# The first norm of a two-layer backbone kernel: its sums in one round, eight modulation steps ahead of the spread, the third product tile joined to the first two, the power tables moved behind

## What is computed

```python
silu_c, silu_cc = jax.nn.silu(c), jax.nn.silu(c_ctx)
ada_lat = silu_c @ ada_w[l] + ada_b[l]            # shift, scale, gate: 6 x 1024 columns
ada_ctx = silu_cc @ ada_w[l] + ada_b[l]
h = rms_norm(x, lp["ln1"]) * (1.0 + sc1) + sh1    # hc alike, for the context tokens
z = h @ w_in                                      # split into attention, Fourier and S5 parts
...
a_bar = jnp.exp(dt * a)                           # S5: discretised states, 24 groups x 64
b_bar = ((a_bar - 1.0) / a)[..., None] * b
s = associative_scan(a_bar, b_bar u)              # the kernel scans chunks of 8 tokens
```

## Time and profile before

| | before |
|---|---|
| median of 3 runs | 2169.61 us (2168.25 to 2172.53) |
| profiled execution, its own time | 2170.0 us |
| its span | 2168.1 us |
| PE busy | 2125.3 us, 98% of the span |
| DVE busy | 1228.1 us, 57% |
| POOL busy | 903.7 us, 42% |
| ACT busy | 505.2 us, 23% |

### The profile page before, as it was taken

How to read it: one execution, slowest core, us unless ns; L and a number is a source line. 1 busy time by engine, 2 the same in 40 slices (tenths; PEclk the granted TensorE clock), 3 DMA queues, 4 the chain that set the end, 5 groups by cost and what they waited for, 6 DMA issues and landing times.

```text
span 2168.1 us, 30631 instructions
## 1 busy us (share of the span) xinstructions
PE 2125.3 (98%) x12532; PEld 1897.7 (88%) x12532; DVE 1228.1 (57%) x1859; ACT 505.2 (23%) x814; POOL 903.7 (42%) x492
## 2 busy tenths in 40 slices
PE   6999999999999999999999999999999999999998
PEld 4999999877799899999999999888777787888886
DVE  7998981455663546454565424594266757263353
ACT  3115121454300220110201111322265212010010
POOL 2441443200243354444444443455411456766662
PEclk9999999999999999999999999999999999999999
DMA  7363354233553332122233254545310552322331
GB/s 282 100 141 101 116 191 145 88 120 120 199 192 138 133 122 88 59 78 88 78 88 103 92 204 187 120 153 195 127 39 23 197 182 88 107 97 97 97 97 68
DMA packets 105390, 267.80 MB, mean 124 GB/s; under 512 B 22650, under 2 KB 42490, under 8 KB 103470
## 3 DMA queue, kind: packets, MB, share of 16 engines
q1 hardware_dynamic: 68928, 190.87, 25.9%
q10 hardware_dynamic: 36334, 75.07, 10.5%
HBM read 227.56 MB, written 37.88 MB: 122 GB/s over the span
## 4 chain that ended last, share of the span: by engine, by line
PE 89%; DVE 8%; DMA 1%; ACT 1%; issue 1%; SPq 0%; POOL 0%; DVEq 0%; POOLq 0%; ACTq 0%
PE ps L482 67%; PE ps L1062 3%; PE ps L936 2%; PE ps L1076 2%; PE ps L1112 2%; PE ps L600 2%; PE ps L491 2%; DVE t_out L2233 2%; DVE t_in L2233 1%; PE ps L795 1%; PE ps L962 1%; PE ps L974 1%; PE ps L497 1%; PE ps L1009 1%; PE ps L925 1%; DMA ada_first<-in_ada_w 1%
## 5 line engine op out<-in xcount | busy, mean ns | idle before, releaser
L1304 POOL TENSOR_SCALAR whi<-raw 128x1024 fp32r<-128x1024 f32 x244 | 273.5, 1121 | 1212.1 <-PE ps L482 665.3
L1307 POOL TENSOR_TENSOR wlo<-raw,whi 128x1024 fp32r<-128x1024 f32 x244 | 630.7, 2585 | 20.3
L482 PE MATMUL ps<-hh,whi 128*128 128x384 f32 (+1 forms) x1560 | 462.8, 353 | 0.3 <-DVE ada L626 0.3
L482 PE MATMUL ps<-hl,whi 128*128 128x384 f32 (+1 forms) x1560 | 460.0, 351 | 0.0
L482 PE MATMUL ps<-hh,wlo 128*128 128x384 f32 (+1 forms) x1560 | 459.8, 351 | 0.0
L482 PEld LDWEIGHTS ps<-hh,whi 128*128 128x128 f32 x1560 | 283.6, 188 | 21.1 <-ACT mr L1737 1.0
L482 PEld LDWEIGHTS ps<-hl,whi 128*128 128x128 f32 x1560 | 285.3, 188 | 18.6 <-issue 0.2
L482 PEld LDWEIGHTS ps<-hh,wlo 128*128 128x128 f32 x1560 | 285.0, 188 | 18.4
L2166 DVE SCALAR_TENSOR_TENSOR x<-ps,ada,x 128x384 f32<-128x384 f32 (+1 forms) x160 | 80.5, 546 | 335.1 <-PE ps L482 335.0
L482 PE MATMUL ps<-midh,whi 128*128 128x384 f32 (+1 forms) x768 | 231.3, 355 | 1.8 <-DVE midl L2196 1.8
L482 PE MATMUL ps<-midl,whi 128*128 128x384 f32 (+1 forms) x768 | 229.7, 353 | 0.0
(11 more groups left out here) (259 smaller groups left out, 2954.9 us busy)
## 6 DMA issues: line engine op xcount, KB each, us to landing
raw<-in_w_main SPq DMA_DIRECT2D x244, 512.0 KB, 3.3
ada_gap<-in_ada_w SPq DMA_DIRECT2D x40, 512.0 KB, 10.1
ada_mixer<-in_ada_w SPq DMA_DIRECT2D x32, 512.0 KB, 4.0
g_d<-gt ACTq DMA_DIRECT2D x24, 384.0 KB, 2.4
gl<-g_d ACTq DMA_DIRECT2D x8, 1152.0 KB, 6.2
ada_first<-in_ada_w SPq DMA_DIRECT2D x16, 512.0 KB, 15.4
cout_d<-cz SPq DMA_DIRECT2D x12, 512.0 KB, 5.0
cout<-cout_d ACTq DMA_DIRECT2D x6, 1024.0 KB, 9.3
```

The source lines that it names most:

```text
L482: ins = pe.matmul(bank(p, h, a, b), ww[:, w % W_SLOTS, kw * P:(kw + 1) * P], xx[:, kx, a:b], start=(first and i == 0 and j == 0), stop=(la ...
L1304: pool.tensor_scalar(whi[:, u, :], raw[:, u % 2, :], 1.0, 0.0, ALU.mult, ALU.add).then_inc(w_split.sem, 1)
L1307: pool.tensor_tensor(wlo[:, u, :], raw[:, u % 2, :], whi[:, u, :].bitcast(F32), ALU.subtract).then_inc(w_split.sem, 1)
```

## The change

1. `pe_first_sums` takes the place of `pe_sums` for the first norm. DVE adds slice 7 into `sqa` too, so six two-column matmuls are left of twelve.
2. Steps 4 to 7 of the modulation all stand between the sums and the spread (before, two stood ahead of the spread and two behind it). `pe_turn` of block 0 stands between the two matmuls of the spread (`pe_first_spread`).
3. Each of the first 16 modulation steps waits for its own load; before, they waited in pairs.
4. Slice 3 is computed for tiles 0 and 1 with `pe_turn(1)` inside it, then slices 0 to 3 for tile 2, then slices 4 to 7 for the three tiles together. Tile 2 is loaded ahead of modulation steps 12 to 15.
5. On DVE, `doubled` by 1 moves behind `invert`; `doubled` by 4 and `inverses` move to between the norm and `inputs`; and all three `inputs` are ahead of `input_weights`.
6. The load of `b_in` (the S5 input weights) moves from the start to behind slice 3 of the norm.
7. Tile 3 has PSUM pair 3 in place of pair 0, and the waits of tiles 3 to 6 and of `halves(0)` follow from that.

```diff
@@ -536,6 +536,24 @@
+        def pe_first_sums(pe):
+
+            key = (0, 1)
+            pe.wait_ge(sq_used.sem, sq_used.at((key, KD - 1)))
+            for b in range(TOK // P):
+                ins = pe.matmul(ps[:, norm_pair(key), 2 * b:2 * b + 2], sqa[:, b * P:b * P + P], ones[:, 0:2],
+                                start=True, stop=True, skip_group_check=True)
+            ins.then_inc(sq_summed.sem, sq_summed.mark(key))
+
+        def pe_first_spread(pe):
+
+            key = (0, 1)
+            pe.wait_ge(diag_ready.sem, diag_ready.at(key))
+            pe.matmul(ps[:, norm_pair(key), 0:512], ones[:, :], diag[:, 0:512], start=True, stop=True)
+            pe_turn(pe, 0)
+            pe.matmul(ps[:, norm_pair(key), 512:TOK], ones[:, :], diag[:, 512:TOK], start=True, stop=True).then_inc(
+                rstd_spread.sem, rstd_spread.mark(key))
...
@@ -595,7 +613,7 @@
             w, slot = ada_slot(s)
-            pe.wait_ge(ada_full[slot].sem, ada_full[slot].at(s | 1 if s < 8 * ADA_FIRST else s))
+            pe.wait_ge(ada_full[slot].sem, ada_full[slot].at(s))
...
@@ -799,32 +817,32 @@
             if l == 0:
-                for k, steps in ((0, range(8, 11)), (1, range(11, 14))):
+                for k, steps in ((0, range(8, 11)), (1, range(11, 13)), (2, range(13, 16))):
                     first_tiles(range(2), k)
                     for s in steps:
                         pe_ada(pe, s)
-                pe.wait_ge(hi_ready.sem, hi_ready.at((0, 1, 2)))
+                pe.wait_ge(hi_ready.sem, hi_ready.at((0, 1, 3)))
                 for i in range(2):
-                    high_step(pe, i, i, 2, TOK)
-                pe_ada(pe, 14)
-                pe_ada(pe, 15)
-                pe.wait_ge(lo_ready.sem, lo_ready.at((0, 1, 2)))
+                    high_step(pe, i, i, 3, TOK)
+                pe_turn(pe, 1)
+                pe.wait_ge(lo_ready.sem, lo_ready.at((0, 1, 3)))
                 for i in range(2):
-                    low_step(pe, i, i, 2, TOK)
-                pe_turn(pe, 1)
-                for k in range(3, KD):
-                    first_tiles(range(2), k)
+                    low_step(pe, i, i, 3, TOK)
+                wait_w(pe, 2)
                 pe.wait_ge(ada_ready.sem, ada_ready.at(1))
-                tile(2, 2)
-                pe.wait_ge(in_dve.sem, in_dve.at((0, 0)))
-                tile(3, 0)
+                for k in range(4):
+                    first_tiles((2,), k)
+                for k in range(4, KD):
+                    first_tiles(range(3), k)
+                tile(3, 3)
                 pe.wait_ge(in_dve.sem, in_dve.at((0, 1)))
                 tile(4, 1)
+                pe.wait_ge(in_act.sem, in_act.at((0, 3)))
                 halves(0)
...
@@ -1252,9 +1267,12 @@
             load_w(1)
-            for step in range(KD, 2 * KD):
+            for step in range(KD, KD + 4):
                 load_ada(step)
-            for t in range(2, n_all):
+            load_w(2)
+            for step in range(KD + 4, 2 * KD):
+                load_ada(step)
+            for t in range(3, n_all):
                 load_w(t)
...
@@ -1367,6 +1385,7 @@
                 for k in range(KD // 2):
                     act_hi(act, 0, 1, TOK, k)
+                act.dma_start(s5[0].b_in[:], A["ssm_b"][0]).then_inc(prep_loaded.sem, prep_loaded.mark(0, 16))
                 act_rows(act, 1)
...
@@ -1860,18 +1878,16 @@
             if l == 0:
                 dve_norm(dve, 0, 1, TOK, 0, KD // 2)
-                doubled(dve, 0, 4)
                 dve_ada(dve, 1)
                 dve_gain(dve, 0, 0, KD // 2, KD)
                 dve_norm(dve, 0, 1, TOK, KD // 2, KD)
-                inputs(0)
-                inputs(1)
+                doubled(dve, 0, 4)
                 inverses(dve, 0)
+                for i in range(3):
+                    inputs(i)
                 input_weights(dve, 0)
                 table_rows(dve, 0)
-                input_tables(dve, 0, 0)
-                inputs(2)
-                for c in range(1, S5_PARTS):
+                for c in range(S5_PARTS):
                     input_tables(dve, 0, c)
...
@@ -2385,11 +2401,11 @@
             coefficients(dve, 0)
-            for k in range(1, KD - 1):
+            for k in range(1, KD):
                 add_squares(dve, (0, 1), k, TOK)
             transition(dve, 0)
+            invert(dve, (0, 1), TOK)
             doubled(dve, 0, 1)
-            invert(dve, (0, 1), TOK)
             doubled(dve, 0, 2)
```

More of the change, by code:

```diff
@@ L81 @@
                 18: (("out", 5), ("kernel", 4), ("kernel", 5))}
-IN_PAIRS = ((0, 1, 2, 0, 1, 2, 0, 1, 2, 0, 1, 0), (0, 1, 2, 0, 1, 2, 0, 1, 0, 2, 3, 1))
+IN_PAIRS = ((0, 1, 2, 3, 1, 2, 0, 1, 2, 0, 1, 0), (0, 1, 2, 0, 1, 2, 0, 1, 0, 2, 3, 1))
 FIRST_GATE = (1, 3)
@@ L579, in ada_slot @@
             if s < 8 * ADA_FIRST:
-                return ada_first[s], s // 2
+                return ada_first[s], s
             s -= 8 * ADA_FIRST
@@ L826, in pe_layer @@
                 halves(1)
-                pe.wait_ge(in_act.sem, in_act.at((0, 3)))
+                pe.wait_ge(in_dve.sem, in_dve.at((0, 0)))
                 tile(6, 0)
@@ L1219, in _ @@
                 pe_ada(pe, s)
-            pe_sums(pe, (0, 1), TOK)
-            pe_ada(pe, 4)
-            pe_ada(pe, 5)
-            pe_spread(pe, (0, 1), TOK)
-            pe_ada(pe, 6)
-            pe_ada(pe, 7)
-            pe_turn(pe, 0)
+            pe_first_sums(pe)
+            for s in range(4, 8):
+                pe_ada(pe, s)
+            pe_first_spread(pe)
             for l in range(DEPTH):
@@ L1445, in act_layer @@
             if l == 0:
-                evacuate(3, zkv[:, 0], 0)
+                evacuate(3, zkv[:, 0], IN_PAIRS[0][3])
                 store_inputs()
@@ L1771, in _ @@
             act.dma_start(early[:], A["early"]).then_inc(early_in.sem, early_in.mark(0, 16))
-            act.dma_start(s5[0].b_in[:], A["ssm_b"][0]).then_inc(prep_loaded.sem, prep_loaded.mark(0, 16))
             act.wait_ge(ones_ready.sem, ones_ready.at(1))
```

## The result

| | median | runs | against before |
|---|---|---|---|
| before | 2170.64 us | 6 (2168.25 to 2172.53) | |
| after | 2179.95 us | 6 (2178.3 to 2183.61) | 1.004 [1.003, 1.005] |

The change makes the kernel 9.3 us slower. The prediction said 2170.5 us, with 2173.8 as the upper end of its range, and gave "slower" 0.09.

What follows compares the result with a forecast made beforehand. TensorE (98% busy) and DVE were taken as level to 161.4 us: 6.6 gained, lost to a 7 us wait (+0.5), plus 1.7 clock, less 1.35 waiting, scan +0.9; 2170.0 became 2170.9, as median 2170.5, range 2166 to 2173.8.

Steps and rivals of the forecast that it cites:

- the end of the three tiles: TensorE's end of tiles 0 to 2, claimed at 60.4 us, 6.6 us earlier than before.
- rival (c): First norm: steps 4 to 7 wait for data or `diag` for POOL, `nt` at 29.5 or later; 2172 us, chance 0.12.
- the 29.9 us of work: TensorE from 30.5 us: three tiles 25.0, eight modulation steps 4.3, the turn 0.6.
- a half-clock stretch: TensorE's first k-steps: 3.4 us at 1.2 GHz after 2.96 us of idling would cost 1.7 us.
- rival (b): Slower by the clock alone: half-clock stretches behind waits, 2173.5 us with two, 2175.2 with a third; chance 0.09.
- The cover of VectorE: `doubled` by 4 and `inverses`, some 5.5 us, run free under TensorE's last k-steps; DVE even idles 1 us.
- The collisions: DVE from copies to `bin` 0: five POOL splits, 2.87 us each, tile 4's only 0.5, on 10.3 us clean work.
- 84.2: Time `bin` 0 is ready, taken between 84.9 with tile 8's split and 82.0 without it.
- The wait at `halves(0)`: TensorE arrives at 77.0 and waits about 7 us for `bin` 0, passing at +0.5 us against before.
- The clock: Behind the wait at `halves(0)`, half clock costs TensorE 1.7 us, with 0 and 3.5 as bounds.
- The store gate: Output table part 3 waits for part 0's store, to 141.8; last table at 163.5, TensorE's 1.35 us wait goes.
- Everything behind keeps its distances: From the scan, starting 0.9 us later, to the end, nothing shifts further, as nothing there reads what was moved.

Runs made afterwards that it cites:

- dve_fill: The changed kernel with `doubled` by 1, 2 and 4 moved between norm slice 3 and `dve_ada(1)`, where VectorE idled for the turn; 2175.89 us.
- norm_fill: norm_only with `doubled` by 1 and 2 moved behind norm slice 3, beside `doubled` by 4; 2172.41 us, 1.0001 of before.
- norm_only: The kernel before with only the first-norm edits (sums, steps ahead of the spread, later `b_in`, `doubled` by 1 behind the inversion); 2169.88 us, 0.999.
- fill_late_in: dve_fill with the three `inputs` copies also moved behind `input_weights`; 2168.2 us, 0.9978 of before.
- thin_splits: The changed kernel with GpSimd's splits of tiles 4 to 7 made on 32 of 1024 columns (products are other numbers); 2167.68 us, 0.9986 of before.
- filler: The changed kernel with sixteen matmuls of constants on TensorE in the wait ahead of `halves(0)`; 2176.75 us, 1.0023 of before.
- late_in: The changed kernel with only the three `inputs` copies moved behind `input_weights`, `doubled` left in place; 2177.26 us, 1.0024 of before.
- norm_warm: norm_fill with six matmuls of constants on TensorE between the spread and the first k-step; 2172.8 us, 1.0003 of before.
- late_warm: fill_late_in with matmuls of constants on TensorE, two ahead of the tiny sums and six between spread and first k-step; 2169.54 us, 0.9992 of before.
- join_only: The kernel before with everything of the change except the first-norm edits (joined third tile, loads, PSUM pairs, DVE order); 2177.37 us, 1.003.

## Why the prediction was wrong

**The step that failed first** is the end of the three tiles, 60.4; it was 64.95. Two terms of it were mis-sized. `nt` was to start with the end of the spread (28.1). It started at 29.81, since I costed steps and spread on TensorE and took VectorE as free, though the code now has `doubled` by 1 and 2 behind the inversion and ahead of `dve_ada(0)`. Clean they would have been hidden under the spread; what was missing is their collision with the split of tile 1, 2.9 us. That was rival (c), with another cause than the two named, and dve_fill shows it, and norm_fill against norm_only. And the 29.9 us of work took 32.7 from 32.25 on: the prediction names a half-clock stretch and its price of 1.7, and leaves it out of the 60.4. There were 6.4 us of it, some 4.7 of them under work, so 2.3. That two stretches of idling (4.07, 7.57) were each followed by a slow one was in rival (b) at 0.09, and should have been in the sum.

**The cover of VectorE.** "Idles 1 us" ahead of the copies was 3.93 for the turn and 1.72 for tile 0. `doubled` by 4 had filled the first gap before. But closing this gap alone only moves the idle time (dve_fill); what counted was that the copies wait for TensorE and hold back the input weights, which don't (fill_late_in).

**The collisions** were right: 22.0 us from the end of the copies to `bin` 0 against 21.6 forecast; clean 10.3 (thin_splits); 2.7 for a full collision in a row of them against 2.87. So of the 5.0 us by which `bin` 0's 89.18 lies behind 84.2, 4.6 are the later start of the copies. I had noted that 82.0 would hold without the split of tile 8 and smoothed the step into a range of 2 us; the runs show it as an edge, with the wait and the clock on its far side.

**The wait at `halves(0)`** was right in size (7.57 for 7), and that it eats the gain. The size is right because both of its ends, TensorE's arrival and `bin` 0, moved back with the three tiles; neither stands where it was forecast. **The clock** behind it cost 2.8 (filler), not 1.7; the upper bound of 3.5 holds it. **The store gate**: VectorE's wait is there as foretold, and 1.35 us of TensorE's waiting shrank only to 0.97. So the scan starts at +5.7 + 2.8 - 0.4 = +8.1 (measured 7.95) where +0.9 stood: 5.2 more at `halves(0)`, 1.1 more of the clock, and 1.0 of waiting that did not go.

**"Everything behind keeps its distances"** is off by 2.4 us in the profiled pair, and it isn't shown that the change does it. The scan's first products end 8.3 us later (183.20 against 174.93). From there to the end after takes 1995.3 us and before 1993.2, and over the thirteen profiles of this case this stretch takes 1991.8 to 1998.6. Granted clocks are 0.94 over 1290 to 1320 and over 1570 to 1600 us in after and 1.00 in before, each 0.06 x 30 = 1.8 us, and 0.97 against 0.94 over 720 to 780, 1.8 the other way. These stretches stand elsewhere in each kernel's profile; fill_late_in has 0.89 over 1290 to 1320 and is the faster one. Why they fall where they do was not tried and stays open, and with it about 1 us of the 9.3. The mean granted clock of whole executions leaves little room for more: 0.9912 over after's six, 0.9945 over the 31 of before that ran beside filler, 0.9948 over filler's ten. The difference of 0.0033 is about 7 us of full clock in 2178, and the two stretches named above account for 6.5 of it (half of 9.9, and half of 6.4 - 3.4), waiting included.

## What to carry to other kernels

When work is joined to shorten TensorE's stretch, look at what the other engine's in-order queue holds behind its wait for that stretch, and put there first what needs nothing of it: this one reordering was the difference between 2175.9 and 2168.2 us, and alone (late_in) worth 2.7. A row of collisions between VectorE and GpSimd is priced well one by one, but ask whether the deadline lies just before or behind the next one, since there the cost has a step. A small operation counts with the split that it may meet, not with its own length. A long wait on TensorE was charged twice here, once as the wait and once as slow clock behind it: 7.57 us brought another 2.8. Shorter ones went either way (in dve_fill a wait of 2.56 us at 28.30 had no slow stretch behind it, one of 2.48 at 44.32 had 6.9 us).

## What the runs showed of the hardware

- An idle stretch filled with products of constants kept the clock (filler: 1.00 over 80 to 100 us against 0.74), but where TensorE then waited at a later place, the clock fell there instead (norm_warm, late_warm), and the time stayed.
- The clock also fell without a long wait: in fill_late_in it is at its lower level from about 21.0 to 34.7 us (0.50 over 22 to 34), and what TensorE did ahead of that was the twelve tiny products (18.84, 1.50 us) and a modulation step, with no wait over 1.2 us.
- The same twelve tiny products at 19 us took 2.72 us in most profiles, 1.80 in dve_fill and 1.50 in join_only and fill_late_in, though the adds ahead of them stand within 0.4 us of one another. The steps beside them change with them (eight matmuls at 16.76 take 0.64 in dve_fill, 1.08 in after), while the granted clock reads 1.00 over 10 to 18 us in both; so this column doesn't explain the start. In join_only `nt` starts at 29.10 by this, 2.55 us ahead of the 31.65 of before, without any edit of the norm. Differences of this size at the start of single profiles have to be read from several runs.
- Copies from PSUM (three in 2.69 us) ran at the same speed beside GpSimd's splits of SBUF as without them, in every kernel here. The Trainium skill (SBUF — State Buffer, "SBUF: two separate sides") describes the shared interface as an exclusive lock for the whole of an instruction, which VectorE contends for when both inputs are in SBUF and GpSimd reads SBUF, or in a two-port mode. For one instruction the trace agrees: in after a `bbz` of 0.56 starts at 69.93 and ends at 72.56, behind GpSimd's `wlo` (69.57 to 72.14). Over a split it is less: 2.7 us of its 3.45 to 3.9, as VectorE gets in between GpSimd's two instructions, which are stretched in turn (`whi` 1.36 for 1.05).
- A tiny split (32 of 1024 columns) costs VectorE next to nothing: four of them left its stretch at the clean 10.3 us.
